# The FFN output product of both layers as seven products of 11 inner tiles

## The chip, the cores and the metric

The kernel runs on one core of one Trainium2 chip. The metric is the device time of one execution in microseconds (us); lower is better. The time before is 2061.62 us, the median of three runs (2058.51 to 2063.2). A difference of 0.2% (about 4 us) is what a measurement of this kernel can tell from no change.

## The reference

A trunk of two decoder layers over 1024 tokens of width 1024, in float32. Layer 0 mixes tokens with a gated spatial unit, layer 1 with windowed attention; each layer ends with the same gated ConvFFN, and the change lies in the last product of that:

```
def conv_ffn(x, g_norm, w_in, conv_w, conv_b, w_out):
    h = rms_norm(x, g_norm)
    hu = causal_depthwise_conv(h @ w_in, conv_w, conv_b)     # 1024 -> 2 x 2816
    gate, up = jnp.split(hu, 2, axis=-1)
    return (jax.nn.silu(gate) * up) @ w_out                  # 2816 -> 1024

x = x + conv_ffn(x, f_norm[layer], f_w_in[layer], ...)       # both layers
```

## The kernel before

Everything is kept transposed, features on the 128 partitions and tokens on the free axis, in two halves of 512 tokens. The 2816 inner features are 22 tiles of 128 (`FT` = 22, `PAIRS` = 11). TensorE (PE) works in float32r, and full precision is had by splitting each operand: ACT copies a tile to its upper part (`hi`), DVE subtracts that from the tile to get the lower part (`lo`), and a product is three matmuls (`three`, L1940 to L1942): hi by hi, hi by lo, lo by hi. Each operand tile therefore costs one ACT copy and one DVE subtraction before PE may use it.

The FFN of a layer has two phases. In the input phase (`body`) the product with `w_in` goes by quads of 2 x 2 blocks, each with seven products instead of eight (Strassen's method in Winograd's form). Per quad POOL makes four sums of weight blocks (`weight_sums`), ACT and DVE split weights, DVE combines the products' banks (`c12`, `u2`, `u3`, `c22`, `c21`), and ACT and DVE apply the convolution (`tap`, `tap_1`, `tap_2`), the gate (`silu`) and their product (`product`). The gated tile goes to DRAM (`c_dram`, `store`), since SBUF has no room for all 22.

The output phase takes each half of the tokens by itself: 11 groups of two inner tiles for half 0, then 11 for half 1. A group loads two weight tiles of 128 x 1024 (`w_f_out`, 1 MB, into `raw`) and two gated tiles (512 KB, into `c_raw`). It makes four weight splits (`out_upper`, `out_lower`) and two token splits (`gated_upper`, `gated_lower`). PE then runs 2 inner tiles x 8 output tiles x 3 = 48 matmuls of 128 x 512 into the eight PSUM banks. When a half is done DVE adds the eight banks to the residual `xT` (`add_f`, L1642), which was saved to `x_dram` and is loaded back. A layer's output phase is 22 x 48 = 1056 matmuls.

Every engine's queue runs in order of the program, and semaphores tie them together. `fw_ready` counts finished weight splits, `c_ready` finished token splits, and `prod_full` PE's steps. `w2` and `p2` are the counts of the first two where the output phase begins. SP issues all DMAs; POOL has no work in the output phase but to scale the weights of the key and value product (`gains`, L606) in layer 0.

Of the kernel before, what the change touches and what calls it, by code (L numbers as in the profile page):

```python
# [63 lines left out]
GROUPS = 2 * PAIRS  # L64
# [24 lines left out]
OUT_SLOT = (0, 1, 2, 3)  # L89
OUT_SLOT_LAST = (4, 6, 5, 0)  # L90
# [8 lines left out]
def sum_at(t, k):  # L99

    return (T1, T3, T2, T4).index(t) * 4 + k + 1

# [41 lines left out]
def build(nc, x_t, w_av, w_au, w_ao, w_f_in, w_f_out, w_kv, w_q, w_o, w_s, b_s, params, c_dram, x_dram, out_t):  # L144
    ctx = ExitStack()
    with ctx:
# [65 lines left out]
        c_raw_1 = sb("c_raw_1", [P, 2, HALF], F32, blk_at[8])  # L212
# [3 lines left out]
        c_raw_0 = sb("c_raw_0", [P, 2, HALF], F32)  # L216
# [6 lines left out]
        out_hi = [fw_hi[0], fw_hi[1], fw_hi[2]]  # L223
        out_lo = [fw_lo[0], fw_lo[1], fw_lo[2]]
        for n, blk in enumerate((10, 10, 13, 13)):
            where = blk_at[blk] + n % 2 * 4 * 4 * P * 2
            out_hi.append(sb(f"out_hi_{n}", [P, SUB], F32R, where)[:, :])
            out_lo.append(sb(f"out_lo_{n}", [P, SUB], F32R)[:, :])
        kv_raw = sb("kv_raw", [P, 2, HB], F32, blk_at[12])
        raw = [raw_1, raw_0]  # L230
        c_raw = [c_raw_0[:, :, :], c_raw_1[:, :, :]]
        c_hi, c_lo = t_hi[B21], t_lo[B21]
# [44 lines left out]
        def weight(q, source):  # L277

            return raw[q][:, RAW[source], :] if source in RAW else w_sum(SUMS.index(source))

# [96 lines left out]
        c_landed = [sem(f"c_landed{s}") for s in range(2)]  # L377
# [3 lines left out]
        x_back = [sem(f"x_back{half}") for half in range(2)]  # L381
# [10 lines left out]
        def _(sp):  # L392
# [62 lines left out]
            def ffn(layer):  # L455
# [9 lines left out]
                def gated(tile, half):  # L465
                    return c_dram[bass.ds(tile, 2), :, half * HALF:(half + 1) * HALF].rearrange("k p t -> p k t")
# [16 lines left out]
                pair0 = layer * PAIRS  # L483
                quad(0, w_f_out[pair0], i * 14 + (w0 + STEADY.index((0, "P3")) + 1))
                for r in range(2):
                    sp.wait_ge(c_stored[r], 16 * (PAIRS * layer + 1))
                sp.dma_start(c_raw[0], gated(d0, 0)).then_inc(c_landed[0], 16)
                store(i - 1, 1)
                store(i - 1, 0)
                quad(1, w_f_out[pair0 + 1], i * 14 + (w0 + STEADY.index((1, "P3")) + 1))  # L490
                sp.wait_ge(prod_full, p2 - 7 + 1)
                for r in range(2):
                    sp.wait_ge(c_stored[r], 16 * (PAIRS * layer + 2))
                sp.dma_start(c_raw[1], gated(d0 + 2, 0)).then_inc(c_landed[1], 16)

                def group(t, g):

                    half = g // PAIRS
                    splits, gates = t * 8 + (w2 + 4 * (g - 1)), t * 4 + (FT * 2 * layer + 2 * (g - 1))
                    weights, src = w_f_out[t * 2 + (pair0 + g % PAIRS)], gated(t * 4 + (d0 + 2 * (g % PAIRS)), half)  # L500
                    sp.wait_ge(fw_ready, splits)
                    sp.dma_start(raw[g % 2][:, :, :].rearrange("p b c -> p (b c)"),
                                 weights).then_inc(raw_landed[g % 2], 16)
                    sp.wait_ge(c_ready, gates)
                    if g < 4:
                        for r in range(2):
                            sp.wait_ge(c_stored[r], 16 * (PAIRS * layer + g + 1))
                    sp.dma_start(c_raw[g % 2], src).then_inc(c_landed[g % 2], 16)

                group(0, 2)  # L510
                store(i, 1)
                store(i, 0)
                group(0, 3)
                for r in range(2):
                    sp.wait_ge(c_stored[r], 16 * PAIRS * (layer + 1))
                for half in range(2):
                    sp.dma_start(xT[:, half, :, :].rearrange("p k t -> p (k t)"),
                                 x_dram[half].rearrange("p k t -> p (k t)")).then_inc(x_back[half], 16)
                if layer == 0:
                    sp.wait_ge(prod_full, p2)  # L520
                    for n in range(2):
                        sp.wait_ge(w_ready[n], use[n].now())
                        sp.dma_start(kv_raw[:, n, :], w_kv[n]).then_inc(w_landed[n], 16)
                        use[n].add()
                with sp.Fori(0, 3) as t:
                    group(t, 4)
                    group(t, 5)
                for g in range(10, 14):
                    group(0, g)
                if layer:  # L530
                    results(0)
                with sp.Fori(0, 4) as t:
                    group(t, 14)
                    group(t, 15)

            def results(half):
                tok = slice(half * HALF, (half + 1) * HALF)
                for dt in range(KT):
                    sp.wait_ge(f_added, 2 * KT + half * KT + dt + 1)
                    sp.dma_start(out_t[dt * P:(dt + 1) * P, tok], xT[:, half, dt, :]).then_inc(out_stored, 16)  # L540
# [9 lines left out]
            results(1)  # L550
# [3 lines left out]
        def _(pool):  # L554
# [34 lines left out]
            def ffn(layer, squares):  # L589

                pool.wait_ge(sq_added, squares)
                weight_sums(layer, 1, 0)
                weight_sums(layer, 1, 1)
                with pool.Fori(2, PAIRS) as i:
                    for q in range(2):
                        weight_sums(layer, i, q)

# [11 lines left out]
            gains(COL_KV_NORM, kv_raw)  # L609
            pool.wait_ge(c_ready, 2 * FT)  # L610
# [74 lines left out]
        def _(act):  # L685
# [190 lines left out]
            def kv_upper(half, k):  # L876

                act.wait_ge(f_added, KT * half + k + 1)
                nc.scalar.activation(h_hi_b[:, k, half * HALF:(half + 1) * HALF], xT[:, half, k, :],
                                     ACT.Copy).then_inc(h_hi_done, 1)  # L880

            def ffn(layer, norm):
# [52 lines left out]
                def body(i, more=True, second=False):  # L935
                    for q in range(2):
# [8 lines left out]
                        elif more:  # L945
                            upper(i, 14)
                        else:
                            out_upper(0, 0, 0)
# [6 lines left out]
                        for m in range(3):  # L955
                            if q == 0:
                                upper(i, 8 + m)
                            elif more:
                                upper(i, 15 + m)
                            else:  # L960
                                out_upper(0, 0, m + 1)
# [4 lines left out]
                        elif more:  # L966
                            upper(i, 18)
                        tap(i, q, 1)

                def out_upper(t, g, u):  # L970

                    act.wait_ge(prod_full, t * 8 + (p2 + 4 * g + u - 3) if g else p2 - RING_F + u + 1)
                    act.wait_ge(raw_landed[g % 2], t * 16 + 16 * (LOADS_F * layer + PAIRS + g // 2 + 1))
                    nc.scalar.activation(out_hi[OUT_SLOT[u]], raw[g % 2][:, u, :], ACT.Copy).then_inc(fw_hi_done, 1)  # L974

                def last_upper(g, u, slot, free):

                    if free:
                        act.wait_ge(prod_full, p2 + free)
                    act.wait_ge(raw_landed[g % 2], 16 * LOADS_F * (layer + 1))  # L980
                    nc.scalar.activation(out_hi[slot[u]], raw[g % 2][:, u, :], ACT.Copy).then_inc(fw_hi_done, 1)

                def gated_upper(t, g, k):
                    act.wait_ge(c_landed[g % 2], t * 16 + 16 * (PAIRS * layer + g // 2 + 1))
                    act.wait_ge(prod_full, t * 8 + (p2 + 4 * (g - 2) + 2 * k + 2) if g >= 2 else p2 - 4)
                    nc.scalar.activation(c_hi[:, 2 * (g % 2) + k, :], c_raw[g % 2][:, k, :],
                                         ACT.Copy).then_inc(c_hi_done, 1)

                def group(t, g):

                    for k in range(2):
                        out_upper(t, g, 2 * k)
                        gated_upper(t, g, k)
                        out_upper(t, g, 2 * k + 1)
# [36 lines left out]
                for k in range(2):  # L1031
                    gated_upper(0, 0, k)
                tap(PAIRS - 1, 1, 0)
                group(0, 1)
                with act.Fori(0, 4) as t:
                    group(t, 2)
                    group(t, 3)
                for g in (10, 11, 12):
                    group(0, g)
                if layer == 0:  # L1040
                    for k in range(KT):
                        kv_upper(0, k)
                    for n in range(2):
                        split_scaled(n, kv_raw)
                with act.Fori(0, 3) as t:
                    group(t, 13)
                    group(t, 14)
                group(0, 19)
                for k in range(2):
# [1397 lines left out]
```

## Time and profile before

| | before |
|---|---|
| median of 3 runs | 2061.62 us |
| time of the profiled execution | 2059.48 us |
| its span, first to last instruction | 2057.7 us |
| mean granted clock of TensorE | 0.99 of full speed |
| busy share of PE, DVE, ACT, POOL | 97%, 68%, 44%, 20% |

The busy share is an average over all stages. The output phases lie at 748.7 to 989.2 us (layer 0) and 1813.7 to 2054.5 us (layer 1) of the span. Times of the trace are from the span's start. The profiled execution took 1.8 us more than its span, and 2.1 us less than the median.

### The profile page before, as it was taken

The numbers are of one execution on the slowest core, as the hardware profiler recorded it, in microseconds if no ns is written. First come the engines' busy times: TensorE is split into PE (matmuls) and PEld (weight loads), VectorE is DVE, ScalarE is ACT, GpSimd is POOL, SyncE is SP. The second block draws the span as 40 slices with busy tenths as digits, with TensorE's granted clock in tenths as the row PEclk, the third lists the DMA queues.
The fourth block names the chain that finished last, engine by engine and source line by source line (L and its number), as shares of the span: only waits on it lengthen the run. The fifth ranks groups of instructions, "written<-read, shape, count | busy, mean of one in ns | idle before, by whom it ended". The sixth has DMA issues, their size and how long they took to land.

```text
span 2057.7 us, 28762 instructions
## 1 busy us (share of the span) xinstructions
PE 1993.5 (97%) x9968; PEld 1688.2 (82%) x9968; DVE 1397.8 (68%) x2030; ACT 912.2 (44%) x1576; POOL 406.0 (20%) x285
## 2 busy tenths in 40 slices
PE   7999899999999999999999799988999999999999
PEld 7988778788888888888999688866888888888887
DVE  5366658888888864453544788889888888853433
ACT  6233435544444443343312778756444444433332
POOL 0000001333333300000110445522333323200000
PEclk9999999999999999999999899999999999999999
DMA  4111232122122245333012000030222222263543
GB/s 168 42 51 41 72 123 102 62 102 82 68 95 82 86 172 222 134 142 143 21 41 72 11 11 22 11 123 30 94 82 82 82 82 82 93 237 140 194 145 110
DMA packets 44729, 193.08 MB, mean 94 GB/s; under 512 B 4336, under 2 KB 4464, under 8 KB 32368
## 3 DMA queue, kind: packets, MB, share of 16 engines
q1 hardware_dynamic: 44656, 192.12, 25.7%
q8 instruction: 44, 0.72, 0.1%
q14 instruction: 29, 0.24, 0.0%
HBM read 156.45 MB, written 35.65 MB: 93 GB/s over the span
## 4 chain that ended last, share of the span: by engine, by line
PE 86%; DVE 9%; ACT 3%; issue 1%; DMA 0%; SPq 0%; POOL 0%; DVEq 0%; ACTq 0%
PE banks L1940 28%; PE banks L1942 27%; PE banks L1941 27%; DVE t_lo L1469 1%; ACT lg L1171 1%; PE banks L2310 1%; DVE t_sum L1661 1%; DVE t_sum L1459 1%; DVE lg L1840 1%; DVE small L1847 1%; PE banks L2284 1%; DVE fw_lo L1451 1%; PE banks L2285 0%; DVE xT L1551 0%; DVE fw_lo L1512 0%
## 5 line engine op out<-in xcount | busy, mean ns | idle before, releaser
L1940 PE MATMUL banks<-t_hi,fw_hi 128*128 128x512 f32 x1760 | 688.0, 391 | 12.7 <-issue 11.0
L1942 PE MATMUL banks<-t_hi,fw_lo 128*128 128x512 f32 x1760 | 686.2, 390 | 0.0
L1941 PE MATMUL banks<-t_lo,fw_hi 128*128 128x512 f32 x1728 | 673.8, 390 | 0.0
L1940 PEld LDWEIGHTS banks<-t_hi,fw_hi 128*128 128x128 f32 x1760 | 331.2, 188 | 86.4 <-issue 14.3
L1942 PEld LDWEIGHTS banks<-t_hi,fw_lo 128*128 128x128 f32 x1760 | 331.1, 188 | 69.1
L1941 PEld LDWEIGHTS banks<-t_lo,fw_hi 128*128 128x128 f32 x1728 | 324.9, 188 | 67.8 <-issue 0.5
L1607 DVE TENSOR_TENSOR fw_lo<-raw,fw_hi 128x512 fp32r<-128x512 f32 x120 | 84.4, 705 | 189.3 <-ACT fw_hi L974 189.3
L581 POOL TENSOR_TENSOR nrm<-raw 128x512 f32<-128x512 f32 x40 | 53.5, 1337 | 749.7 <-DVE fw_lo L1512 439.2
L927 ACT ACTIVATE xT<-xT,par 128x1024 f32<-128x1024 f32 x88 | 109.3, 1245 | 161.5 <-DVE xT L1538 119.0
L974 ACT ACTIVATE fw_hi<-raw 128x512 fp32r<-128x512 f32 x120 | 75.6, 631 | 210.7 <-PE banks L1942 210.7
L1551 DVE SCALAR_TENSOR_TENSOR xT<-xT,par 128x1023 f32<-128x1023 f32 x88 | 151.3, 1720 | 0.0
L901 ACT ACTIVATE fw_hi<-nrm 128x512 fp32r<-128x512 f32 x160 | 100.0, 626 | 78.9 <-PE banks L1942 78.9
L1512 DVE TENSOR_TENSOR fw_lo<-raw,fw_hi 128x512 fp32r<-128x512 f32 x120 | 121.6, 1013 | 18.8 <-ACT fw_hi L901 18.8
L1512 DVE TENSOR_TENSOR fw_lo<-nrm,fw_hi 128x512 fp32r<-128x512 f32 x160 | 109.9, 688 | 21.3 <-ACT fw_hi L901 17.8
L1256 DVE TENSOR_TENSOR w_lo<-w_raw,w_hi 128x1024 fp32r<-128x1024 f32 x43 | 55.5, 1291 | 101.3 <-ACT w_hi L696 53.8
L1558 DVE SCALAR_TENSOR_TENSOR xT<-xT,par 128x1022 f32<-128x1022 f32 x88 | 116.1, 1319 | 0.3
L1940 PE MATMUL banks<-w_hi,h_hi_b 128*128 128x256 f32 x384 | 108.8, 283 | 0.0
L1942 PE MATMUL banks<-w_hi,h_lo_b 128*128 128x256 f32 x384 | 108.7, 283 | 0.0
L1941 PE MATMUL banks<-w_lo,h_hi_b 128*128 128x256 f32 x384 | 108.7, 283 | 0.0
L1940 PE MATMUL banks<-h_hi_a,w_hi 128*128 128x512 f32 x256 | 101.5, 396 | 7.3 <-DVE nrm L1393 4.0
L587 POOL TENSOR_TENSOR nrm<-nrm,raw 128x512 f32<-128x512 f32 x40 | 86.4, 2159 | 81.0 <-DVE fw_lo L1512 80.3
L1941 PE MATMUL banks<-h_lo_a,w_hi 128*128 128x512 f32 x256 | 100.7, 393 | 0.0
(183 smaller groups left out, 3645.6 us busy)
## 6 DMA issues: line engine op xcount, KB each, us to landing
raw<-in_w_f_in SPq DMA_DIRECT2D x44, 1024.0 KB, 4.8
raw<-in_w_f_out SPq DMA_DIRECT2D x44, 1024.0 KB, 4.8
c_scratch<-xT SPq DMA_DIRECT2D x44, 512.0 KB, 2.6
c_raw<-c_scratch SPq DMA_DIRECT2D x44, 512.0 KB, 5.6
w_raw<-in_w_ao SPq DMA_DIRECT2D x16, 512.0 KB, 3.5
x_scratch<-xT SPq DMA_DIRECT2D x4, 2048.0 KB, 7.2
xT<-x_scratch SPq DMA_DIRECT2D x4, 2048.0 KB, 12.8
xT<-in_x_t SPq DMA_DIRECT2D x16, 256.0 KB, 7.2
```

The costliest lines, as they stand in the source:

```text
L587: nc.gpsimd.tensor_tensor(w_sum(3), w_sum(1), a12, ALU.add).then_inc(sums_done, 1)
L901: nc.scalar.activation(fw_hi[n % RING_F], weight(q, source), ACT.Copy).then_inc(fw_hi_done, 1)
L927: nc.scalar.activation(y_row(q, r), z_row(q, r), ACT.Identity, bias=par[:, bass.ds(tile + (conv + 6 * FT), 1)], scale=par[:, bass.ds(tile ...
L974: nc.scalar.activation(out_hi[OUT_SLOT[u]], raw[g % 2][:, u, :], ACT.Copy).then_inc(fw_hi_done, 1)
L1256: nc.vector.tensor_tensor(w_lo[:, slot, :], src[:, slot, :], w_hi[:, slot, :].bitcast(F32), ALU.subtract).then_inc(w_ready[slot], 1)
L1512: nc.vector.tensor_tensor(fw_lo[n % RING_F], weight(q, PRODUCTS[p][0]), fw_hi[n % RING_F].bitcast(F32), ALU.subtract).then_inc(fw_ready, 1)
L1551: link(nc.vector.scalar_tensor_tensor(out=y[:, 1:T], in0=z[:, 0:T - 1], scalar=par[:, bass.ds(i * 2 + (q * FT + r + conv + 2 * FT), 1)], i ...
L1558: nc.vector.scalar_tensor_tensor(out=y[:, 2:T], in0=z[:, 0:T - 2], scalar=par[:, bass.ds(i * 2 + (q * FT + r + conv), 1)], in1=y[:, 2:T], ...
L1607: nc.vector.tensor_tensor(out_lo[OUT_SLOT[u]], raw[g % 2][:, u, :], out_hi[OUT_SLOT[u]].bitcast(F32), ALU.subtract).then_inc(fw_ready, 1)
L1940: nc.tensor.matmul(out, w_h, m_h, start=start, stop=False, **kw)
L1941: nc.tensor.matmul(out, w_h, m_l, start=False, stop=False, **kw)
L1942: return nc.tensor.matmul(out, w_l, m_h, start=False, stop=stop, **kw)
```

## The change

The output product is treated as 2 x 2 blocks as well. The inner features are cut in two halves of 11 tiles, the output features in two of 512 and the tokens in two of 512. Weight blocks are A11, A12, A21, A22 and token blocks b11, b12, b21, b22. Seven products replace eight. Each has 11 steps; a step is one inner tile into four banks, 12 matmuls. That makes 77 steps and 924 matmuls per layer, 132 fewer. Products alternate between two sets of four banks (`BANKS_U`, `BANKS_V`), P6 and P7 go on in the banks of the product before, and DVE adds or subtracts each finished product into one or two blocks of `xT` (`out_add`, 36 per layer instead of 16).

Each step needs one weight split and one token split: 77 and 77 per layer, where there were 88 and 44. The ring of tokens has three slots and that of weights five.

The gated blocks are now kept in SBUF whole, and DVE makes 44 token sums in place (`token_sum`). POOL makes 44 sums of weights (`out_sums`). POOL also issues their transfers itself: 11 bases of up to 1 MB in three groups for S1, three more for S3, and 44 single tiles of 256 KB into the ring `raw_0`. SP loads the unsummed weights tile by tile (`direct`, 33), the token blocks in groups of 4, 4 and 3 tiles (`tokens`, 12), and the residual in four parts (`back`). The weights of the key and value product go back to `w_raw` and are loaded once POOL's sums are done; POOL's constants for the attention (L612 to L620) wait for the end of the output phase. The loops of the output phase are written out.

```diff
+OUT_STEPS = ("P2", "P1", "P5", "P6", "P4", "P7", "P3")
+OUT_DIRECT = {0: (0, A12), 1: (PAIRS, A11), 4: (2 * PAIRS, A22)}
+OUT_SUMMED = {2: 1, 3: PAIRS + 1, 6: 2 * PAIRS + 2}
+OUT_TARGETS = (((0, 0, 1),), ((0, 0, 1),), ((1, 0, -1), (1, 4, 1)), ((1, 0, 1),), ((0, 4, 1),),
+               ((0, 4, -1), (1, 4, -1)), ((1, 0, 1),))
+TOKEN_GROUPS = ((0, 4), (4, 8), (8, PAIRS))
...
+                tokens("b11", 0)
+                direct(7)
+                direct(8)
                 store(i, 1)
+                direct(9)
+                direct(10)
                 store(i, 0)
+                direct(11)
                 for r in range(2):
                     sp.wait_ge(c_stored[r], 16 * PAIRS * (layer + 1))
+                tokens("b21", 2)
+                direct(12)
+                tokens("b11", 1)
+                direct(13)
+                tokens("b11", 2)
+                direct(14)
+                back(0, 0)
+                direct(15)
+                tokens("b12", 0)
...
+            def out_sums(layer):
...
+                def stage(e):
+                    k, b = addend(e)
+                    if e >= 4:
+                        pool.wait_ge(w_added, first + e - 3)
+                    nc.gpsimd.dma_start(raw_0[:, e % 4, :], w_f_out[layer * PAIRS + k][:, b * SUB:(b + 1) * SUB]
+                                        ).then_inc(e_landed[e % 4], 16)
+                def add(e):
+                    k, b = addend(e)
+                    g = min(k // 4, 2)
+                    to = (b21 if b == A21 else a_sum)[:, k, :]
+                    if b == A22:
+                        pool.wait_ge(a_landed[g], 16 * (layer + 1))
+                    elif b == A11:
+                        pool.wait_ge(fw_ready, w2 + 2 * PAIRS + k + 1)
+                    elif b == A21:
+                        pool.wait_ge(s3_landed[g], 16 * (layer + 1))
+                    else:
+                        pool.wait_ge(fw_ready, w2 + 3 * PAIRS + k + 1)
+                    pool.wait_ge(e_landed[e % 4], 16 * (PAIRS * layer + e // 4 + 1))
+                    nc.gpsimd.tensor_tensor(to, to, raw_0[:, e % 4, :], ALU.add).then_inc(w_added, 1)
+
+                pool.wait_ge(prod_full, p2 - 4)
+                for g in range(3):
+                    base(a_sum, g, A21, a_landed)
+                pool.wait_ge(fw_ready, w2)
+                for e in range(3):
+                    stage(e)
+                for e in range(4 * PAIRS):
+                    if e + 3 < 4 * PAIRS:
+                        stage(e + 3)
+                    if e in (2 * PAIRS, 2 * PAIRS + 8, 2 * PAIRS + 16):
+                        g = (e - 2 * PAIRS) // 8
+                        pool.wait_ge(token_summed, 4 * PAIRS * layer + 2 * PAIRS + TOKEN_GROUPS[g][1])
+                        base(b21, g, A11, s3_landed)
+                    add(e)
...
+                def gated_upper(n):
+                    s, k = n // PAIRS, n % PAIRS
+                    if n < 2:
+                        act.wait_ge(prod_full, p2 - 6 + n)
+                    elif n >= 3:
+                        act.wait_ge(prod_full, p2 + n - 2)
...
+                def out_phase():                                     # on DVE
+                    i = PAIRS - 1
+                    c12(i, 1, p2)
+                    out_lower(3)
+                    tap_1(i, 1, 1)
+                    tap_2(i, 1, 1)
+                    product(i, 1)
+                    gated_lower(3)
+                    out_lower(4)
+                    tap_1(i, 1, 0)
+                    gated_lower(4)
+                    tap_2(i, 1, 0)
+                    out_lower(5)
+                    product(i, 0)
+                    for m in range(2, STEPS):
+                        if 2 < m < STEPS - 2:
+                            gated_lower(m + 2)
+                            token_sum(m + 2)
+                        if m >= PAIRS and 1 <= m % PAIRS <= 4:
+                            out_add(m // PAIRS - 1, m % PAIRS - 1)
+                        n = split_at(m)
+                        if n is not None and n < STEPS:
+                            out_lower(n)
+                        if m >= TAIL:
+                            beside(m - TAIL)
+                    for d in range(4):
+                        out_add(6, d)
...
+                def out_step(n):                                     # on PE
+                    s, k = n // PAIRS, n % PAIRS
+                    hi, lo = out_slot(n)
+                    pe.wait_ge(fw_ready, w2 + n + 1)
+                    pe.wait_ge(c_ready, c0 + n + 1)
...
```

`split_at(m)` is m + 4 up to step 64, then m + 3. `token_sum(n)` does something for steps n = 11 to 54. A11 adds make S2, A21 adds S3 (in `b21`, whose tokens are used up by then) and A12 adds S4.

## Rows read from the trace of the kernel before

**Rows 1.** The page: span and part 1, busy us, share, instructions.
```profile
span 2057.7 us, 28762 instructions
PE 1993.5 (97%) x9968; PEld 1688.2 (82%) x9968; DVE 1397.8 (68%) x2030; ACT 912.2 (44%) x1576; POOL 406.0 (20%) x285
```

**Rows 2.** Busy time by windows, both output phases: us, engines' busy (instructions), clock, DMA, GB/s.
```profile
core 0: us, PE busy (x) PEld busy (x) DVE busy (x) ACT busy (x) POOL busy (x), PEclk, DMA share, GB/s
748.66:988.90 240.24, 239.63 (x1055) 197.81 (x1056) 113.13 (x164) 86.34 (x145) 10.92 (x23) 1.00 0.43 158
1813.70:2054.60 240.90, 240.21 (x1056) 197.96 (x1056) 101.13 (x151) 76.15 (x128) 0.00 (x0) 1.00 0.44 162
```

**Rows 3.** Waits of PE from 700 to 1010 us: total us, times, longest.
```profile
PE banks L1940 <- DVE t_lo L1619: 0.6, 1, 0.6
```

**Rows 4.** Timeline of PE: start us, us, what; first and last of 1056, and the next.
```profile
749.25 0.50 PE L1940 MATMUL banks<-t_hi,fw_hi 128*128 128x512 f32 x1 [0.59 <-DVE t_lo L1619]
...
989.09 0.39 PE L1942 MATMUL banks<-t_hi,fw_lo 128*128 128x512 f32 x1
989.32 0.28 PE L1940 MATMUL banks<-w_hi,h_hi_b 128*128 128x256 f32 x1
```

**Rows 5.** Single lines of DVE, ACT: ns min/median/max, first and last start.
```profile
L1619 DVE TENSOR_TENSOR t_lo<-c_raw,t_hi x88: 681/684/2379, 748.5 to 2033.8; 128x512 fp32r<-128x512 f32 x88
L986 ACT ACTIVATE t_hi<-c_raw x88: 612/616/633, 747.9 to 2032.9; 128x512 fp32r<-128x512 f32 x88
L1642 DVE TENSOR_TENSOR xT<-banks,xT x32: 678/688/692, 868.4 to 2054.6; 128x512 f32<-128x512 f32 x32
L1519 DVE TENSOR_TENSOR xT<-banks,xT x40: 678/683/686, 373.3 to 1800.4; 128x512 f32<-128x512 f32 x40
```

**Rows 6.** Timeline of DVE after the output phase of layer 0 begins.
```profile
750.31 1.27 DVE L1551 SCALAR_TENSOR_TENSOR xT<-xT,par 128x1023 f32<-128x1023 f32 x1
751.62 1.28 DVE L1558 SCALAR_TENSOR_TENSOR xT<-xT,par 128x1022 f32<-128x1022 f32 x1
...
756.85 1.22 DVE L1567 TENSOR_TENSOR xT<-xT 128x1024 f32<-128x1024 f32 x1
757.99 0.68 DVE L1607 TENSOR_TENSOR fw_lo<-raw,fw_hi 128x512 fp32r<-128x512 f32 x1
758.59 0.68 DVE L1619 TENSOR_TENSOR t_lo<-c_raw,t_hi 128x512 fp32r<-128x512 f32 x1
```

**Rows 7.** Timeline of POOL in a quad of the input phase.
```profile
672.55 1.29 POOL L583 TENSOR_TENSOR nrm<-nrm,raw 128x512 f32<-128x512 f32 x1
673.80 1.74 POOL L584 TENSOR_TENSOR nrm<-raw 128x512 f32<-128x512 f32 x1
677.60 2.18 POOL L587 TENSOR_TENSOR nrm<-nrm,raw 128x512 f32<-128x512 f32 x1 [2.05 <-DVE fw_lo L1512]
```

**Rows 8.** Timeline of DVE beside it.
```profile
673.14 1.25 DVE L1512 TENSOR_TENSOR fw_lo<-raw,fw_hi 128x512 fp32r<-128x512 f32 x1
674.32 2.31 DVE L1551 SCALAR_TENSOR_TENSOR xT<-xT,par 128x1023 f32<-128x1023 f32 x1
...
678.55 0.68 DVE L1519 TENSOR_TENSOR xT<-banks,xT 128x512 f32<-128x512 f32 x1
679.15 1.18 DVE L1512 TENSOR_TENSOR fw_lo<-raw,fw_hi 128x512 fp32r<-128x512 f32 x1
```

**Rows 9.** The queue of SP: an issue; and issues by line with time to landing.
```profile
715.46 0.35 SPq L448 DMA_DIRECT2D raw<-in_w_f_out  x1
...
raw<-in_w_f_out SPq DMA_DIRECT2D x44, 1024.0 KB, 4.8
c_scratch<-xT SPq DMA_DIRECT2D x44, 512.0 KB, 2.6
```

**Rows 10.** Other operations of POOL.
```profile
969.97 1.39 POOL L615 TENSOR_SCALAR_AFFINE_SELECT dist<-dist 128x128 f32<-128x128 f32 x1
971.32 0.74 POOL L617 TENSOR_SCALAR_AFFINE_SELECT dist<-dist 128x128 f32<-128x128 f32 x1
```

**Rows 11.** Busy time by windows of 4 us, while the residual comes back.
```profile
768.00:772.00 4.00, 4.00 (x19) 3.34 (x18) 1.29 (x2) 1.79 (x3) 0.00 (x0) 1.00 1.02 435
```

More of the change, by code:

```diff
@@ L101, in sum_at, with added, final, ring_uses @@
     return (T1, T3, T2, T4).index(t) * 4 + k + 1
+def added(s, d):
+    return max(i + 1 for i, a in enumerate(OUT_ADDS) if a[:2] == (s, d))
+def final(half, dt):
+    return max(i + 1 for i, a in enumerate(OUT_ADDS) if a[2:4] == (half, dt))
+def ring_uses(r, m):
+    return len([i for i in range(m) if i % 4 == r])
+def split_at(m):
+    if m == TAIL - 1:
+        return None
+    return m + 4 if m < TAIL - 1 else m + 3
 def norm_at(norm):
@@ L376, in build @@
         c_stored = [sem(f"c_stored{r}") for r in range(2)]
-        c_landed = [sem(f"c_landed{s}") for s in range(2)]
+        d_landed = [sem(f"d_landed{s}") for s in range(4)]
+        b_landed = {b: [sem(f"{b}_landed{g}") for g in range(3)] for b in ("b11", "b12", "b21", "b22")}
+        a_landed = [sem(f"a_landed{g}") for g in range(3)]
+        s3_landed = [sem(f"s3_landed{g}") for g in range(3)]
+        e_landed = [sem(f"e_landed{g}") for g in range(4)]
+        w_added = sem("w_added")
+        token_summed = sem("token_summed")
         c_hi_done = sem("c_hi_done")
@@ L380, in build @@
         x_saved = [sem(f"x_saved{half}") for half in range(2)]
-        x_back = [sem(f"x_back{half}") for half in range(2)]
+        x_back = [[sem(f"x_back{half}{dh}") for dh in range(2)] for half in range(2)]
         t_scaled = sem("t_scaled")
@@ L482, in ffn @@
                 i = PAIRS - 1
[L483 to L487, printed above, removed]
+                sp.wait_ge(fw_ready, i * 14 + (w0 + STEADY.index((0, "P3")) + 1))
+                for m in range(4):
+                    direct(m)
                 store(i - 1, 1)
@@ L489, in ffn @@
                 store(i - 1, 0)
-                quad(1, w_f_out[pair0 + 1], i * 14 + (w0 + STEADY.index((1, "P3")) + 1))
-                sp.wait_ge(prod_full, p2 - 7 + 1)
+                sp.wait_ge(prod_full, p2 - 5)
                 for r in range(2):
[L493 to L508, printed above, removed]
@@ L510, in ffn @@
-                group(0, 2)
+                    sp.wait_ge(c_stored[r], 16 * (PAIRS * layer + 8))
+                tokens("b21", 0)
+                sp.wait_ge(prod_full, p2 - 3)
+                for r in range(2):
+                    sp.wait_ge(c_stored[r], 16 * (PAIRS * layer + 10))
+                tokens("b21", 1)
+                for m in (4, 5, 6):
+                    direct(m)
+                sp.wait_ge(prod_full, p2)
+                tokens("b11", 0)
+                direct(7)
+                direct(8)
@@ L519, in ffn @@
+                tokens("b22", 1)
+                direct(22)
+                back(1, 0)
+                direct(23)
+                back(1, 1)
+                direct(24)
+                tokens("b22", 2)
+                direct(25)
+                back(0, 1)
+                if layer:
+                    for dt in range(4):
+                        result(0, dt)
+                for m in range(26, 3 * PAIRS):
+                    direct(m)
                 if layer == 0:
-                    sp.wait_ge(prod_full, p2)
+                    sp.wait_ge(w_added, 4 * PAIRS)
@@ L536, in results @@
[L536 to L540, printed above, removed]
+                        load(n, w_kv[n])
+                if layer:
+                    for half in range(2):
+                        for dt in range(4, KT):
+                            result(half, dt)
+                    for dt in range(4):
+                        result(1, dt)
@@ L976, in last_upper @@
[L976 to L987, printed above, removed]
@@ L1030, in ffn @@
                 body(PAIRS - 1, False)
[L1031 to L1049, printed above, removed]
-                    last_upper(20, 2 * k, OUT_SLOT, 77 + 2 * k)
-                    gated_upper(0, 20, k)
-                for k in range(2):
-                    last_upper(21, 2 * k, OUT_SLOT_LAST, 0)
-                    gated_upper(0, 21, k)
-                for k in range(2):
-                    last_upper(20, 2 * k + 1, OUT_SLOT, 78 + 2 * k)
-                for k in range(2):
-                    last_upper(21, 2 * k + 1, OUT_SLOT_LAST, 81 * k)
+                out_phase()
             ffn(0, 1)
```

396 lines of the change are left out of this document (209 added, 187 removed).

## The prediction

> **What bounds the kernel now.** I read the page first, then the windows of the two output phases, then what PE waited for in them, and only then single instructions. PE is busy 97% of the span [rows 1]. That share is an average, so the windows matter more: in both output phases PE is busy for all but 0.6 us of 240, at full clock, while DVE works 113 and 101 us, ACT 86 and 76, POOL 11 and 0 [rows 2]. The reader should see that PE alone sets the end there and that POOL is free. The one wait of PE in the phase is the 0.6 us at its start, for a token split [rows 3, 4]. So a matmul that is not run gives its whole time back as long as the operands still come in time.
>
> The pace is (989.32 - 749.25) / 1056 = 0.2273 us per matmul, with the slow first one; the steady spacing is 0.2267. Eight products are 240 us a layer. A step of the new phase, 12 matmuls, is 2.72 us.
>
> **What it removes.** 132 matmuls per layer: 132 x 0.2267 = 29.9 us. The first step needs only banks whose adds are done earlier, and its token split is ahead of `c12`, so I give the 0.6 us at the start back too. Together -30.5 us a layer, -61 us in all, if nothing new waits.
>
> **What it adds, by engine.**
> - PE: nothing.
> - ACT: 154 copies of 0.62 us [rows 5] in 77 steps, 1.24 us of each 2.72. Hidden.
> - DVE: 77 + 77 splits and 44 token sums, all with two inputs in SBUF, at 0.60 us from start to start (757.99 to 758.59) [rows 6], and 36 adds from PSUM at the same price. (154 + 44 + 36) x 0.6 = 140 us of 209.5. As a sum it fits. By step: two splits 1.2; with a token sum 1.8; with one add 2.4; with two adds (after P5, four steps) 3.0, over the 2.72. DVE's token split for step m + 2 can begin about 1.0 us into step m (semaphore and ACT copy) and takes 0.7, so DVE may fall 5.4 - 1.7 = 3.7 us behind before PE waits. Four steps at 3.0 use 1.2 of that. Alone, DVE would hold.
> - POOL: 44 adds and 50 DMA issues. An undisturbed add is 1.29 us [rows 7].
> - The moved constants of POOL (about 3 us) and the later start of the last eight token splits for the key and value product (four more after the end, 2.4 us) lie beside that product's first columns: nothing.
>
> **Where POOL and DVE meet** [rows 7, 8]. DVE's split begun at 673.14 takes 1.25 us instead of 0.68 and ends 0.55 after POOL's add has ended (673.84). POOL's next add takes 1.74: it waits for that split. The tap behind it, begun at 674.32, takes 2.31 instead of 1.27 and ends 1.1 after POOL's end (675.54). The add at 677.60 again waits for a tap. Yet DVE's add from PSUM at 678.55, inside that POOL add, takes 0.68, and all 40 such are within 686 ns [rows 5]. So an operation of DVE with two SBUF inputs and an add of POOL exclude each other and take turns, and PSUM adds are free of it. Each POOL add takes about 1.2 us from DVE wherever DVE has work queued. Of the new phase's DVE work only the 36 adds are exempt.
>
> **The price of a POOL issue** is in no row: SP issued all DMAs before. Below, it can cost what SP's issue does, 0.35 us [rows 9]; above, POOL would be held for the whole landing of such a transfer, no more than the 4.8 us of 1 MB. Nearest are POOL's own operations over 128 elements a partition, 0.74 and 1.39 us [rows 10]; I take 1.1 us for a tile and 2 us for a base of four tiles. (The Trainium skill, "DMA: Bandwidth & Descriptors", section "SWDGE vs HWDGE vs iDMA", says that POOL's cores build each descriptor of such a transfer in software, and its latency table gives about 1 us to the first byte. No row shows it; with 1.0 us the sum would be the same to 1 us.)
>
> **Start of the phase**, T0 = PE's first output matmul. POOL may go at four steps before (T0 - 10.9): three bases to -4.9, three tiles to -1.6, one more, first add near T0 - 0.4. A cycle is issue 1.1, the end of DVE's operation, add 1.2: about 2.4 us. The first 11 adds have all they need and run freely until T0 + 27. DVE's queue there, in order: token split 2, `c12`, split 3, two taps, product, token split 3, split 4, tap, token split 4, tap, split 5, product, split 6, token split 5. Taps and products 1.2 each [rows 6], others 0.6: 12.6 us. Without POOL token split 5 ends near T0 + 13 and PE wants it for step 5 at 13.6: 0.6 us of room. With POOL one tap or two short operations fit between adds, and stepping through the list gives eight and a half adds among them: token split 5 ends at T0 + 22.9. PE is 9.3 us late at step 5. Behind it the last gated tile is ready at 20.5, is stored (2.6 us [rows 9]) after split 6, and `tokens("b21", 2)` goes out near 26 and lands near 30, for step 8 at 31: just in time. The first b12 group is behind some 4 MB, at 435 GB/s at best [rows 11], and lands near 39; DVE waits for it some 3 us, inside its 3.7. I take 9 us for the start. The ends: with 0.35 us per issue all 11 adds fall in, 11 x 1.2 - 0.6, about 12 us; with 2 us per tile and 3 per base the first add is at T0 + 6, three fall in, about 3 us.
>
> **Middle.** Adds 11 to 21 (S2) follow DVE's splits one by one: 1.8 + 1.2 = 3.0 us a step for 11 steps, and four PSUM adds that partly overlap, 3 + 1.5 us, against 3.7 of room: 1 us. From step 37, adds 22 to 37 (S3, S4) come in two free runs of eight, 20 us each, and take 9.6 us each: DVE needs 1.8 of 2.72 us and gets half, 3 us behind in each, with P5's adds before them (1.2) and P6's beside them (4 x 0.6): 1 to 2 us. Together 2.5; ends 0 (if PSUM adds and POOL overlap well) and 6.
>
> **Last S3 sum.** From step 36.8, 21 cycles and two base waits of 1.6 steps put add 42 at 36.8 + 3.2 + 21 x 0.88 = step 58.6; PE needs it by 64.4. The cover is gone when a cycle is over 3.16 us, an issue of about 1.8.
>
> **Sum.** Per layer -30.5 + 9 + 2.5 = -19.0; two layers -38.0. Span 2057.7 - 38.0 = 2019.7, profiled execution 2021.5, and with the median's 2.1 us above it 2023.6: 2024 us.
>
> **The rivals.**
> 1. *Cover holds.* POOL's adds fall where DVE idles, stalls under 3 us a layer: 2061.6 - 2 x 29 = 2003 or a little less. For it: DVE's sum is 140 of 209 us and the 3.7 us of room. Against: 0.6 us of room at step 5, before which DVE has no idle time, and the taking of turns [rows 7, 8]. 22%.
> 2. *POOL bounds P7.* Issue of 2 to 2.7 us: cycle 3.5 to 4.2; each us over 3.16 costs 21 us a layer, 7 to 22, start 3, middle 1. Net -19 to -5 a layer: 2024 to 2052. Nothing in the trace excludes it. 16%.
> 3. *Slower, by the same mechanism.* From 21 x (c - 3.16) + 3 = 30.5 the even point is c = 4.5, an issue of 3.0 us. At 3.3, c = 4.8: 34 + 3 - 30.5 = 7 us a layer, 2075. For it only the upper bound, the landing time. 5%.
> 4. *Transfers late.* Some 7 MB around T0 through one queue: b21's second group or b12 some 5 us later than above, on top of my forecast: 2034. For it, 435 GB/s is the top seen and residual, tokens and tiles share it. 7%.
>
> My forecast has 50%. Its own range is 2010 to 2034 (stalls of 5 to 17 us a layer). For 8 in 10: down to rival 1 and into rival 2: 2002 to 2043. Within 0.2% (4 us) 2%, slower 5%, faster 93%. The Trainium skill's "SBUF — State Buffer", section "Who interferes with whom", says of the shared port that the later one blocks fully for the whole instruction and that issue order decides who waits. By it alone POOL's adds could win every turn, the 12 us end: 2030. The trace agrees with full blocking (2.31 us for a tap of 1.27).
>
> **What the profile should show.** 924 matmuls a phase at 0.2267 apart; PE waits for DVE's token split about T0 + 8 to T0 + 23, in both layers alike, 9 us; splits of 1.2 to 1.9 us there and POOL adds of 1.3 to 2.4; few waits between steps 44 and 55; none for `w_added` at P7. DMA issues of about 1 us on POOL. It is wrong if those issues are much under 0.5 or over 1.8 us, if POOL's first adds wait for their landing until after T0 + 10, or if splits stay at 0.68 beside POOL's adds.

## The result and the profile after

The changed kernel takes 2082.57 us (median of 4 runs, 2081.0 to 2084.73) where the kernel before took 2062.41 beside it (4 runs): a ratio of 1.0101, interval 1.0084 to 1.0119. It is slower by 1%. The forecast was 2024, range 2002 to 2043, with 5% for slower.

The page of the kernel after, span and part 1, against [rows 1]:

```profile
span 2083.0 us, 28195 instructions
PE 1965.8 (94%) x9704; PEld 1657.3 (80%) x9704; DVE 1604.6 (77%) x2202; ACT 934.0 (45%) x1620; POOL 590.7 (28%) x473
```

The 264 matmuls are gone (9968 to 9704), but PE is busy only 28 us less, and idle 53 us more. Both output phases of the kernel after, in the windows of [rows 2]:

```profile
752.01:1002.44 250.43, 223.76 (x925) 180.44 (x924) 211.19 (x245) 95.35 (x163) 94.25 (x89) 0.94 0.46 159
1827.73:2079.62 251.89, 224.82 (x925) 181.00 (x923) 202.34 (x235) 86.80 (x150) 85.53 (x87) 0.94 0.47 162
```

They take 250.4 and 251.9 us instead of 240.2 and 240.9, 21.2 us of the span's 25.3 more. The rest is mostly a later start of the first phase (752.01 against 748.66). That varies between executions: in the runs below it lies between 747.0 and 753.2. 924 matmuls at 0.2267 are 209.5 us, so 41 us of the first phase are something else. PE's waits from 735 to 1020 us:

```profile
PE banks L2104 <- DVE fw_lo L1778: 26.7, 10, 6.6
```

26.7 us are waits for DVE's token split (L1778, `gated_lower`; the weight split is L1773, `out_lower`). What is left, 250.4 - 209.5 - 26.7 = 14.2 us, is in the matmuls themselves, which don't keep 0.2267. DVE is busy 211 us with 245 operations, which take 159 where POOL adds nothing (experiment 1): the same operations last longer. The two timelines at the start of the phase, DVE first, then POOL:

```profile
761.29 2.26 DVE L1773 TENSOR_TENSOR fw_lo<-raw,fw_hi 128x512 fp32r<-128x512 f32 x1
763.47 2.77 DVE L1704 SCALAR_TENSOR_TENSOR xT<-xT,par 128x1023 f32<-128x1023 f32 x1
766.28 1.63 DVE L1778 TENSOR_TENSOR fw_lo<-b,fw_hi 128x512 fp32r<-128x512 f32 x1
767.84 2.78 DVE L1711 SCALAR_TENSOR_TENSOR xT<-xT,par 128x1022 f32<-128x1022 f32 x1
...
776.60 2.23 DVE L1778 TENSOR_TENSOR fw_lo<-b,fw_hi 128x512 fp32r<-128x512 f32 x1
```
```profile
755.06 1.29 POOL L726 TENSOR_TENSOR a_sum<-a_sum,raw 128x512 f32<-128x512 f32 x1 [8.89 <-DMA raw<-in_w_f_out]
...
761.11 0.56 POOL L709 DMA_DIRECT2D raw<-in_w_f_out  x1 [0.30 <-POOL a_sum L726]
761.69 1.30 POOL L726 TENSOR_TENSOR a_sum<-a_sum,raw 128x512 f32<-128x512 f32 x1
763.29 0.56 POOL L709 DMA_DIRECT2D raw<-in_w_f_out  x1 [0.30 <-POOL a_sum L726]
763.86 1.29 POOL L726 TENSOR_TENSOR a_sum<-a_sum,raw 128x512 f32<-128x512 f32 x1
```

POOL runs a fixed cycle: add 1.30, gap 0.30, issue 0.56, next add, 2.15 to 2.23 us in all, 2.17 in most. In each cycle DVE finishes one operation, whatever its length: a split takes up to 2.26 instead of 0.68 and a tap 2.77 instead of 1.27. POOL's eleven adds stay at 1.27 to 1.36 us, so all of the waiting is on DVE's side. Token split 5 ends at 778.83, T0 + 26.8. PE starts on it at 778.98:

```profile
778.98 0.76 PE L2104 MATMUL banks<-fw_hi,fw_hi 128*128 128x512 f32 x1 [6.63 <-DVE fw_lo L1778]
779.54 0.63 PE L2105 MATMUL banks<-fw_lo,fw_hi 128*128 128x512 f32 x1
779.97 0.63 PE L2106 MATMUL banks<-fw_hi,fw_lo 128*128 128x512 f32 x1
...
784.60 0.40 PE L2105 MATMUL banks<-fw_lo,fw_hi 128*128 128x512 f32 x1
784.83 0.40 PE L2106 MATMUL banks<-fw_hi,fw_lo 128*128 128x512 f32 x1
```

The windows of the same stretch (the third number from the end is the granted clock):

```profile
779.00:781.00 2.00, 2.00 (x5) 1.61 (x6) 2.00 (x4) 0.00 (x0) 0.13 (x1) 0.50 0.90 319
...
785.00:787.00 2.00, 2.00 (x10) 1.62 (x10) 0.00 (x0) 0.00 (x0) 0.00 (x0) 1.00 0.91 336
```

Behind the wait of 6.63 us the granted clock is 0.50, the lower level of 1.2 GHz, and matmuls start 0.43 apart. After about 5.3 us it rises to 1.00 again, and they are 0.23 apart. In the first phase 50 matmuls in six groups start about 0.43 apart, each group shortly behind a wait of 1.9 us or more: 50 x 0.20 = 10 us. Behind a seventh such wait (2.53 us, up to 939.76) none is slow. Most of the other 4 us lies right at the ten waits: 1.8 behind them, where the first matmul takes 0.56 to the next start (four times) or 0.31 (six times) instead of 0.23, and 1.7 in front, where the last matmul counts until its own end.

Two kinds of wait come without POOL's adds as well (experiments 3 and 4). DVE's first token sum of b12, then ACT's copies at the start and at `tokens("b21", 2)`:

```profile
803.44 0.69 DVE L1787 TENSOR_TENSOR b<-b,b 128x512 f32<-128x512 f32 x1 [8.13 <-DMA b<-c_scratch]
```
```profile
758.80 0.63 ACT L1141 ACTIVATE fw_hi<-raw 128x512 fp32r<-128x512 f32 x1 [4.10 <-DMA raw<-in_w_f_out]
...
789.45 0.63 ACT L1155 ACTIVATE fw_hi<-b 128x512 fp32r<-128x512 f32 x1 [12.68 <-DMA b<-c_scratch]
```

The wait for b12 costs PE 3.41 us (until 805.49), that for b21's last group 0.94 (until 790.95). Later, in S3 and S4, DVE and POOL starve each other in turn. DVE, then POOL:

```profile
929.77 1.15 DVE L1778 TENSOR_TENSOR fw_lo<-b,fw_hi 128x512 fp32r<-128x512 f32 x1 [0.56 <-ACT fw_hi L1155]
930.85 2.28 DVE L1797 TENSOR_TENSOR b<-b,b 128x512 f32<-128x512 f32 x1
933.05 5.97 DVE L1773 TENSOR_TENSOR fw_lo<-b,fw_hi 128x512 fp32r<-128x512 f32 x1
```
```profile
924.93 5.44 POOL L726 TENSOR_TENSOR b<-b,raw 128x512 f32<-128x512 f32 x1 [6.70 <-DMA b<-in_w_f_out]
...
933.44 1.30 POOL L726 TENSOR_TENSOR b<-b,raw 128x512 f32<-128x512 f32 x1
934.68 1.32 POOL L726 TENSOR_TENSOR a_sum<-a_sum,raw 128x512 f32<-128x512 f32 x1
935.93 1.31 POOL L726 TENSOR_TENSOR b<-b,raw 128x512 f32<-128x512 f32 x1
937.18 1.28 POOL L726 TENSOR_TENSOR a_sum<-a_sum,raw 128x512 f32<-128x512 f32 x1
```

POOL's add at 924.93 ends at 930.37: its 1.3 us fall behind seven DVE operations of 0.68 back to back, from where DVE stood idle (929.21 to 929.77). DVE's split at 933.05 lasts through four POOL adds that stand back to back. These four are the last adds of the layer, the only ones with no issue between them. It is no accident of one run: a DVE operation of 5.92 to 5.97 us stands beside them in both layers here and in both layers of experiments 7 and 8, and nowhere in experiment 2, where no add has an issue behind it. Why the turns are not kept in these places no row shows. PE waits 11.0 us in five waits between 886 and 940, the last of them, 2.53 us, behind that split. Layer 1 waits in the same three stretches; both phases together have 53.7 us in 19 waits.

### The profile page after: what moved, and what is told of

The parts are those of the page before. It is cut to its first block, busy times and chain, and to the rows that moved or that the text cites. A ratio compares the mean times of both kernels' runs of the same rounds, so it can differ in the third digit from the quotient of the medians.

```text
span 2083.0 us, 28195 instructions
## 1 busy us (share of the span) xinstructions
PE 1965.8 (94%) x9704; PEld 1657.3 (80%) x9704; DVE 1604.6 (77%) x2202; ACT 934.0 (45%) x1620; POOL 590.7 (28%) x473
## 4 chain that ended last, share of the span: by engine, by line
PE 72%; DVE 19%; ACT 3%; DMA 3%; issue 2%; SPq 0%; POOL 0%; DVEq 0%; ACTq 0%
PE banks L2104 23%; PE banks L2105 23%; PE banks L2106 23%; DVE fw_lo L1778 3%; DVE fw_lo L1773 3%; DMA b<-c_scratch 2%; DVE t_lo L1622 1%; ACT lg L1324 1%; DVE b L1797 1%; PE banks L2440 1%; DVE t_sum L1862 1%; DVE xT L1814 1%; DVE b L1791 1%; DVE b L1794 1%; DVE xT L1704 1%
## 5 line engine op out<-in xcount | busy, mean ns | idle before, releaser
L2104 PE MATMUL banks<-t_hi,fw_hi 128*128 128x512 f32 x1248 | 488.8, 392 | 11.5 <-issue 11.1
L2106 PE MATMUL banks<-t_hi,fw_lo 128*128 128x512 f32 x1248 | 486.8, 390 | 0.0
L2105 PE MATMUL banks<-t_lo,fw_hi 128*128 128x512 f32 x1216 | 474.6, 390 | 0.0
L2104 PE MATMUL banks<-fw_hi,fw_hi 128*128 128x512 f32 x544 | 224.0, 412 | 53.7 <-DVE fw_lo L1778 53.7
L2105 PE MATMUL banks<-fw_lo,fw_hi 128*128 128x512 f32 x544 | 220.9, 406 | 0.0
L2106 PE MATMUL banks<-fw_hi,fw_lo 128*128 128x512 f32 x544 | 220.4, 405 | 0.0
L1778 DVE TENSOR_TENSOR fw_lo<-b,fw_hi 128x512 fp32r<-128x512 f32 x154 | 135.7, 881 | 72.3 <-ACT fw_hi L1155 72.1
L2104 PEld LDWEIGHTS banks<-fw_hi,fw_hi 128*128 128x128 f32 x544 | 107.8, 198 | 86.1 <-issue 49.3
L2106 PEld LDWEIGHTS banks<-fw_hi,fw_lo 128*128 128x128 f32 x544 | 107.6, 198 | 23.8
L2105 PEld LDWEIGHTS banks<-fw_lo,fw_hi 128*128 128x128 f32 x544 | 108.0, 199 | 22.4
```

The costliest lines, as they stand in the source:

```text
L1778: nc.vector.tensor_tensor(tok_lo[n % 3], out_token(n), tok_hi[n % 3].bitcast(F32), ALU.subtract).then_inc(c_ready, 1)
L2104: nc.tensor.matmul(out, w_h, m_h, start=start, stop=False, **kw)
L2105: nc.tensor.matmul(out, w_h, m_l, start=False, stop=False, **kw)
L2106: return nc.tensor.matmul(out, w_l, m_h, start=False, stop=stop, **kw)
```

## The experiments

All start from the kernel after unless they say otherwise. Each time is a median of four runs (of ten for the seventh). The ratio is to the kernel before, which ran beside at 2063.06 (first four) and 2063.26 (last four). "Phase" is layer 0's output phase in the profile, "waits" PE's idle time in it, "slower" the phase less 209.5 less the waits. The profiled execution is one of the four and lies up to 6 us from their median (experiment 3: 2007.90).

| kernel | median us | ratio (interval) | phase | waits | slower |
|---|---|---|---|---|---|
| after | 2082.57 | 1.0101 (1.0084 to 1.0119) | 250.4 | 26.7 | 14.2 |
| 1 no adds | 2019.75 | 0.9801 (0.9781 to 0.9821) | 220.6 | 7.5 | 3.6 |
| 2 adds, few issues | 2051.34 | 0.9944 (0.9925 to 0.9962) | 237.4 | 17.9 | 10.0 |
| 3 bases only | 2013.76 | 0.9768 (0.9752 to 0.9785) | 214.1 | 4.2 | 0.4 |
| 4 sums on DVE | 2018.84 | 0.9798 (0.9774 to 0.9823) | 220.9 | 8.8 | 2.6 |
| 5 and tokens first | 2008.93 | 0.9741 (0.9723 to 0.9759) | 215.8 | 4.2 | 2.1 |
| 6 and bases later | 2016.82 | 0.9775 (0.9758 to 0.9792) | 218.7 | 6.8 | 2.4 |
| 7 first adds later | 2063.74 | 1.001 (0.9997 to 1.0023) | 239.3 | 19.9 | 9.9 |
| 8 small issues | 2074.85 | 1.0064 (1.0039 to 1.0089) | 241.7 | 23.7 | 8.5 |

**1. POOL's adds left out, its issues kept.**

```diff
-nc.gpsimd.tensor_tensor(to, to, raw_0[:, e % 4, :], ALU.add).then_inc(w_added, 1)
+pool.sem_inc(w_added, 1)
```

> POOL issues all its transfers but its 44 adds per layer are left out (a semaphore increment stands in; the summed weights are thus unsummed). If POOL's adds are what holds DVE up: DVE's splits go back to 0.68 us, PE waits under 10 us in all, about 2010 us. If POOL's issues themselves hold DVE (after, only one DVE operation fitted into a POOL cycle of 2.2 us, 0.56 of it issue), splits beside them stay long and 2020 to 2030. If late transfers at the start of the phase are the cause: all the waits near steps 8 and 12 stay, about 2055 or more.

2019.75 us: the adds cost 63 us, more than the whole gain. An issue alone slows nothing: in layer 0's phase two short DVE operations last over 0.69 us (1.48 and 2.38, at 901.67 and 903.08), and both stand beside POOL's scaling of the key and value weights. DVE, then POOL, in this kernel:

```profile
760.21 0.68 DVE L1773 TENSOR_TENSOR fw_lo<-raw,fw_hi 128x512 fp32r<-128x512 f32 x1
760.82 1.22 DVE L1720 TENSOR_TENSOR xT<-xT 128x1024 f32<-128x1024 f32 x1
```
```profile
760.46 1.12 POOL L709 DMA_DIRECT2D raw<-in_w_f_out  x2 [1.02 <-DMA raw<-in_w_f_out]
```

**2. Only the first four tiles staged, and all adds read those.**

```diff
-pool.wait_ge(e_landed[e % 4], 16 * (PAIRS * layer + e // 4 + 1))
+pool.wait_ge(e_landed[e % 4], 16 * (layer + 1))
...
-if e + 3 < 4 * PAIRS:
+if e + 3 < 4:
```

> POOL's adds stay, but only the first four tiles are loaded into its ring and every later add reads one of these (wrong sums): no tile issue between adds. If the add alone holds DVE, 1.25 us each, adds now follow one another and DVE gets still less turns at the start and in the runs of eight: 2060 to 2085, single DVE operations of several us. If the issues between adds are what makes a turn cost 1.6 us instead of 1.25: 2040 to 2055. If transfers are the cause, 22 MB fewer of them: 2030.

2051.34 us. Without an issue between two adds the two engines still alternate one for one, but a turn with a short DVE operation is 1.70 us instead of 2.17, and now POOL's adds are held too (1.74 us). DVE, then POOL:

```profile
900.83 1.77 DVE L1773 TENSOR_TENSOR fw_lo<-raw,fw_hi 128x512 fp32r<-128x512 f32 x1
902.52 1.75 DVE L1778 TENSOR_TENSOR fw_lo<-b,fw_hi 128x512 fp32r<-128x512 f32 x1
```
```profile
900.32 1.74 POOL L726 TENSOR_TENSOR a_sum<-a_sum,raw 128x512 f32<-128x512 f32 x1
902.01 1.72 POOL L726 TENSOR_TENSOR b<-b,raw 128x512 f32<-128x512 f32 x1
```

So 40 issues a layer and their 10 MB are worth 31 us beside the adds, though by experiments 1 and 3 they are worth 6 us without them.

**3. Neither adds nor tile issues; only the six bases.** As 1, and `stage` is never called.

> No adds and no tile issues on POOL; only the six group transfers per layer stay (weights unsummed). What the seven products cost without POOL's part: contention theory 2003 us, within 5 us of the sum without stalls; if tokens and residual come too late by themselves, PE still waits some 10 us per layer near steps 8 and 12: 2025 or more.

2013.76 us. PE waits for a token split here, in this kernel L1773, at step 8 and step 12:

```profile
773.12 0.47 PE L2099 MATMUL banks<-fw_hi,fw_hi 128*128 128x512 f32 x1 [1.37 <-DVE fw_lo L1773]
787.05 0.46 PE L2099 MATMUL banks<-fw_hi,fw_hi 128*128 128x512 f32 x1 [2.81 <-DVE fw_lo L1773]
```

The seven products are worth 49 us as soon as nothing disturbs DVE. The 4.2 us of waits in layer 0 (3.1 in layer 1) come from transfers alone: ahead of them ACT waits 6.8 us for b21's last group and DVE 7.5 for b12.

**4. All 44 sums on DVE, nothing left out.** POOL keeps its issues; the order is S1, S2, all of S3, S4.

```diff
+def weight_sum(e):                        # on DVE, with the waits that POOL's add had
+    ...
+    nc.vector.tensor_tensor(to, to, raw_0[:, e % 4, :], ALU.add).then_inc(w_added, 1)
...
+for s, at in enumerate((6, 20, 42, 53)):  # in DVE's loop over steps m
+    if at <= m < at + PAIRS:
+        weight_sum(s * PAIRS + m - at)
```

> All of the computation, the 44 sums per layer made by DVE (0.60 us each, at steps 6, 20, 42 and 53 on) from the same tiles, POOL only issues. DVE's work rises to 167 of 209 us, at most 3.0 us in a step. Contention theory: no DVE operation over 1.3 us, PE waits under 5 us per layer, 2005 to 2012. If DVE's own load is the bound, stalls near steps 12 to 16, 23 to 26 and 45 to 48: 2020 to 2030. If transfers are the cause: 2050 or more.

2018.84 us. The engine that I had wanted to relieve carries the sums at 0.68 us each, as cheap as if they were not there: experiment 1, which has the same traffic and no sums, took 2019.75. What is left is one wait of 6.32 us for b12 (DVE waited 9.6 us for the transfer), 1.56 at step 8 and 0.95 at step 5. Experiment 1 waits elsewhere, 6.07 of its 7.5 us at step 8 for b21, so that the two times agree to 1 us is in part luck; that DVE's operations stay at 0.68 is not.

**5. As 4, with b12 further ahead in SP's queue.** The first group of b12 goes out right behind b21's last, ahead of b11's second; its second group goes ahead of b11's third. (The diff is against experiment 4.)

```diff
 tokens("b21", 2)
 direct(12)
-tokens("b11", 1)
+tokens("b12", 0)
 direct(13)
-tokens("b11", 2)
-direct(14)
 back(0, 0)
+direct(14)
+tokens("b11", 1)
...
```

> The version with the sums on DVE, but SP issues the first b12 group right behind b21's last one, then the residual's first part, and the b11 groups 1 and 2 later. There PE stood 6.3 us at step 12 behind DVE, which waited 9.6 us for b12. If that order is the cause the wait at step 12 goes in both layers and the time falls 8 to 12 us, to about 2008. If the transfers are simply too many for the stretch another wait takes its place (step 15 or so) and the time stays within 3 us of 2019.

2008.93 us (2007.21 to 2011.11), faster than both kernels. Windows of its two phases, and DVE while it makes S1:

```profile
747.92:963.71 215.79, 211.37 (x925) 172.91 (x924) 183.24 (x289) 94.72 (x163) 27.94 (x45) 1.00 0.52 184
1788.74:2004.35 215.61, 211.32 (x925) 172.81 (x923) 175.11 (x279) 86.42 (x150) 23.82 (x43) 1.00 0.54 190
```
```profile
774.53 0.68 DVE L1754 TENSOR_TENSOR fw_lo<-b,fw_hi 128x512 fp32r<-128x512 f32 x1
775.13 0.68 DVE L1749 TENSOR_TENSOR fw_lo<-raw,fw_hi 128x512 fp32r<-128x512 f32 x1
775.74 0.68 DVE L1807 TENSOR_TENSOR a_sum<-a_sum,raw 128x512 f32<-128x512 f32 x1
```

DVE is busy 183 us with 289 operations, against 211 with 245 in the kernel after, and the granted clock is 1.00 in both phases.

**6. As 5, with the bases of S1 issued from two steps into the phase on.** The tiles of S1 go with them, and its sums start at step 9.

```diff
-pool.wait_ge(prod_full, p2 - 4)
-for g in range(3):
-    base(a_sum, g, A21, a_landed)
+if e in (0, 4, 8):                        # in the loop over tiles
+    pool.wait_ge(prod_full, p2 + 2 + 5 * e // 4)
+    base(a_sum, e // 4, A21, a_landed)
```

> As the one before, and the group transfers of S1 and its tiles are issued by POOL from two steps into the phase on instead of four steps ahead of it, the S1 sums at steps 9 to 19. If these 2.8 MB are what made ACT wait 3.7 us for the directly loaded tile at the start and PE 0.9 us at step 4, that wait goes: 2 to 4 us less than the run before, about 2005. If they now meet tokens and residual, PE waits near steps 8 to 14 come back: 2010 or more.

2016.82 us, worse than 5 by 8. The short waits at steps 3 to 5 are gone, but b21's last group comes 3 us later (ACT uses it 27.3 us into the phase, in experiment 5 24.1), and PE waits 6.84 us behind it at step 8 instead of 2.03. PE's waits, then ACT's, of this kernel:

```profile
PE banks L2098 <- DVE fw_lo L1753: 6.8, 1, 6.8
```
```profile
ACT fw_hi L1130 <- DMA b<-c_scratch: 8.0, 1, 8.0
```

The bases have to move somewhere; before the phase is the better place of the two.

**7. The kernel after, with the first 11 adds held until steps 6 to 16.**

```diff
 if b == A22:
     pool.wait_ge(a_landed[g], 16 * (layer + 1))
+    pool.wait_ge(prod_full, p2 + 6 + k)
```

> The changed kernel with one wait more: POOL's first eleven adds wait for steps 6 to 16 to be done, one per step, so they leave DVE alone while it still has the taps and gate products of the last tiles. Contention theory: the waits of PE before step 8 (11 us a layer) go, and with them part of the low clock after them; those of the middle stay: 2050 to 2062. If it is the transfers at the start that are late, little changes: 2078 or more.

2063.74 us, the time of before. The waits up to step 5 shrink from 11.4 us to 1.3, and the one at step 8, for b21, grows from 0.94 to 2.10. The wait for b12 grows to 7.35, since DVE is ahead and the transfer is not (DVE waits 11.5 us for it), and the middle still has 9.2 us in five waits (878.96 to 923.65). A kinder schedule of POOL's adds gives 19 us back and leaves the rest.

**8. The kernel after, with all tiles but the first four cut to 32 bytes per partition.**

```diff
-nc.gpsimd.dma_start(raw_0[:, e % 4, :], w_f_out[...][:, b * SUB:(b + 1) * SUB]
+c = SUB if e < 4 else 8
+nc.gpsimd.dma_start(raw_0[:, e % 4, 0:c], w_f_out[...][:, b * SUB:b * SUB + c]
```

> The changed kernel with every tile issue of POOL after the first four cut to 32 bytes of each partition (wrong sums): the issues are still there between the adds, the 22 MB are not. The version with adds and no issues took 2051, the changed kernel 2083. If the issue between two adds belongs to POOL's turn (DVE gets one operation per cycle of 2.2 us, not of 1.7), this stays at 2075 to 2083. If the traffic made the difference, 2051 to 2058.

2074.85 us, much nearer to the kernel after than to experiment 2. The turn is still 2.18 us with almost no bytes. DVE, then POOL:

```profile
903.25 2.27 DVE L1798 TENSOR_TENSOR b<-b,b 128x512 f32<-128x512 f32 x1
905.45 0.67 DVE L1815 TENSOR_TENSOR xT<-xT,banks 128x512 f32<-128x512 f32 x1
```
```profile
903.66 1.31 POOL L727 TENSOR_TENSOR a_sum<-a_sum,raw 128x512 f32<-128x512 f32 x1
905.26 0.55 POOL L710 DMA_DIRECT2D raw<-in_w_f_out  x1 [0.29 <-POOL a_sum L727]
905.84 1.31 POOL L727 TENSOR_TENSOR b<-b,raw 128x512 f32<-128x512 f32 x1
```

Of the 31 us between experiment 2 and the kernel after, 23.5 are the issue that stands between two adds, and 8 the bytes. The add from PSUM beside it keeps its 0.67.

## Why the prediction was wrong

**Right.** The removed matmuls are worth what I said: PE alone set the phase, and with POOL's adds gone the time falls by 49 to 54 us of the 61 (experiments 3 and 5). PSUM adds are exempt from the turns. POOL's cycle is 2.17 us where I had 2.4 (an issue is 0.55 where I had 1.1, and 0.76 to 0.79 for a base where I had 2), and ACT never waits for `w_added`, so the bound on the last S3 sum holds and rival 2 falls. Rival 1 falls too: the waits are 27 us a layer, not under 3. Both layers stall alike, first at the start of the phase.

**The step that failed: what DVE gets between two adds of POOL.** I wrote that each POOL add takes about 1.2 us from DVE and that "one tap or two short operations fit between adds". That was read from two neighbouring operations of [rows 8], where DVE and POOL met by chance. With both queues full DVE gets one operation per POOL cycle, long or short. A tap loses 0.9 us by it (2.17 instead of 1.27), a short operation 1.57 (2.17 instead of 0.60). Between two adds lie 0.30 + 0.56 = 0.86 us, and a second short operation does not fit: the one that was held takes 0.56 of them (762.99 to 763.55), and the next is held through the coming add although it began 0.39 us ahead of it (763.47 against 763.86).

- At the start I had eight and a half adds among DVE's list, token split 5 at T0 + 22.9 and PE 9.3 us late. The list met all 11 adds, the split ended at T0 + 26.8, and PE waited 11.4 us up to step 5. Eleven operations, five long and six short, took eleven cycles; by my rule two pairs of short ones would have shared a cycle, 4.3 us less. The loss per add was near my 1.2 here, since half of the list is long (the eleven took 23.6 us, and by the starts in experiment 7, where nothing holds them, 9.8: 1.25 each). What I had too small was the number of adds. The first add began at T0 + 3.05, not T0 - 0.4, which by itself helped DVE.
- In the middle I had 2.5 us; it was 11.0. There all operations under the turns are short. In a free run of eight adds (17.4 us, 6.4 steps) DVE gets 8 operations where these steps need 19, so DVE falls 11 x 0.6 = 6.6 us behind, not 3. That is past its room of 3.7, and each of the two runs makes PE wait 4.2 us. The last six adds, 38 to 43, I had not priced at all; they cost the 2.53 us at step 54. The adds of S2, where I had 1 us, cost nothing.
- Experiment 4 shows the cause from the other side: take the adds from POOL and give DVE 44 more operations a layer, and 64 us come back.

None of my three signs of being wrong appeared: issues took 0.55 us, the first add came before T0 + 10, and splits beside adds did not stay at 0.68. No sign asked how many operations fit into a cycle. The durations that I had named for the start did differ: splits up to 2.26 us instead of 1.9, POOL adds at most 1.36 instead of 2.4.

**Not priced: what a wait does to TensorE afterwards.** I took the matmuls at 0.2267 throughout. Behind each of six waits 5 to 12 of them go at 0.43 and a granted clock of 0.50, 10 us in layer 0, and with what is lost right at the waits 14.2, more than half of the waits themselves. In the table "slower" follows the waits: 10.0 us beside 17.9, 2.1 beside 4.2. No run separates the clock from the waits, so this is read from the timelines and windows, not isolated.

**Transfers late** (rival 4, 7%) is true beside the main cause. I had b12 inside DVE's 3.7 us of room; DVE waited 8.1 us for it, and PE 3.41, and another 0.94 at b21. Experiment 5 removes the b12 wait by the order of the queue alone and gains 10 us over experiment 4 (both layers). The residual 4.2 us a layer there are 2.0 at b21, 1.1 at the start and 1.1 at step 15, behind a directly loaded tile of weights for which ACT waits: a small wait in the place of the large one. The two traces don't say how much of the first two is the bases' 2.8 MB and how much the store of the last gated tiles; experiment 6 shows only that the bases do worse inside the phase.

The account of layer 0, as the difference between forecast and measurement: 29.2 us (+10.2 instead of -19.0). Start up to step 5: 11.4 - 9 = 2.4. b21 and b12: 4.4. Middle: 11.0 - 2.5 = 8.5. Slower matmuls: 14.2, the largest term, and most of it follows the waits of the other three. Sum 29.5.

Rival 3, the only one on the slower side, asked for issues of 3 us or more; they took 0.55. The range missed the time because every branch counted a stall as its own length and let DVE have what POOL's adds left over. The Trainium skill, "SBUF — State Buffer", section "Who interferes with whom", says that the order of issue decides who blocks. Read as "POOL could win every turn" it gave me 2030; the traces show neither side winning while both have work, but an alternation, with exceptions to either side (5.97 and 5.44 us above).

## What to carry to other kernels

Count work with two SBUF operands on DVE and POOL as one shared resource: here, while POOL's queue was full, each such DVE operation lasted a whole POOL cycle, including the transfer that POOL issued between its adds. Here 44 sums a layer were nearly free on the busier engine (0.68 us each) and cost 63 us on the idle one. Count operations per cycle, not time: short operations lose the most. Price a stall of TensorE above its own length: in these traces each microsecond of waiting brought 0.36 to 0.56 of one more around it, mostly in slower matmuls, where the waits were over 15 us a layer. When a product gets shorter, reorder its loads as well: the tokens that are first summed must be first in the queue.

## What the runs showed of the hardware

- While both have work queued, DVE's two-SBUF operations and POOL's adds alternate one for one: a turn with a short DVE operation is 1.70 us with adds alone and 2.17 with an issue of 0.55 between them; a tap of 1.27 lasts 2.77. An add from PSUM beside them keeps 0.67.
- The issue of a transfer holds POOL for 0.55 us (256 KB or 4 KB alike), and DVE's operations beside it, with no add behind it, keep 0.68 and 1.22 us. The mean over the kernel after, all issues of tiles and of the first bases:

```profile
L709 POOL DMA_DIRECT2D raw<-in_w_f_out x88 | 48.8, 555 | 23.8 <-POOL a_sum L726 18.4 <-POOL b L726 5.4
...
L697 POOL DMA_DIRECT2D a_sum<-in_w_f_out x6 | 4.7, 789 | 40.6 <-PE banks L2106 40.6
```

- Either side can be starved: one DVE operation lasted through the four POOL adds that had no issue between them (5.92 to 5.97 us, in both layers of the kernel after and of experiments 7 and 8), and one POOL add through seven DVE operations (5.44 us).
- After a wait of 6.6 us TensorE's granted clock stood at 0.50 for about 5.3 us of full work. It fell behind waits of 1.92 and 2.31 us too, and not behind one of 2.53.
